# Expert down product as three fp32r products: hidden rows and down weights split in two parts, output gate weights loaded after the experts

## The reference

```
def swiglu(x, w_gate, w_up, w_down):
    return (jax.nn.silu(x @ w_gate) * (x @ w_up)) @ w_down
```

## Time and profile before

| | us |
|---|---|
| median of three runs | 1937.7 (1934.84 to 1939.48) |
| profiled execution | 1947.41 |
| its span | 1945.4 |
| PE busy | 1769.4 (91%) |
| DVE busy | 940.4 (48%) |
| ACT busy | 785.6 (40%) |
| POOL busy | 469.5 (24%) |

### The profile page before, as it was taken

How to read it: one execution, slowest core, us unless ns; L and a number is a source line. 1 busy time by engine, 2 the same in 40 slices (tenths; PEclk the granted TensorE clock), 3 DMA queues, 4 the chain that set the end, 5 groups by cost and what they waited for, 6 DMA issues and landing times. The chain is left out here.

```text
span 1945.4 us, 26491 instructions
## 1 busy us (share of the span) xinstructions
PE 1769.4 (91%) x7429; PEld 1131.6 (58%) x7430; DVE 940.4 (48%) x1605; ACT 785.6 (40%) x1460; POOL 469.5 (24%) x592
## 2 busy tenths in 40 slices
PE   7999999978997899989999988999999999866997
PEld 4666666535875666666666655666665666543443
DVE  2333333314685444554445453553555535537885
ACT  2222222212422555555555564554555545541221
POOL 0010000003662232333323323222223232320110
PEclk9999999978998999989999998999999999887999
DMA  9200000022154887887787887787888877857651
GB/s 358 76 0 0 0 0 0 24 85 98 34 132 120 256 265 225 275 282 231 239 246 237 247 252 236 236 251 225 254 245 257 257 236 216 277 194 329 258 184 38
DMA packets 158985, 358.80 MB, mean 184 GB/s; under 512 B 31858, under 2 KB 46002, under 8 KB 156365
## 3 DMA queue, kind: packets, MB, share of 16 engines
q1 hardware_dynamic: 122981, 285.78, 47.8%
q0 software_dynamic: 35328, 72.27, 10.5%
q10 hardware_dynamic: 640, 0.28, 0.1%
HBM read 330.19 MB, written 68.98 MB: 205 GB/s over the span
## 5 line engine op out<-in xcount | busy, mean ns | idle before, releaser
L194 DVE TENSOR_TENSOR lo_gu<-raw_gu,hi_gu 128x1024 fp32r<-128x1024 f32 x260 | 317.5, 1225 | 535.1 <-ACT hi_gu L188 531.5
L1257 PE MATMUL B<-raw_d,hT 128*128 128x512 f32 (+1 forms) x768 | 367.1, 630 | 55.0 <-ACT hT L1367 33.2
L188 ACT ACTIVATE hi_gu<-raw_gu 128x1024 fp32r<-128x1024 f32 x260 | 275.1, 1061 | 189.9 <-PE B L1207 189.9
L1207 PE MATMUL B<-hi_gu,x_hi 128*128 128x512 f32 (+1 forms) x768 | 327.7, 427 | 3.0 <-issue 3.0
L1093 POOL DMA_INDIRECT y_dram<-y,put x128 | 141.0, 1101 | 719.3 <-issue 376.7
L1207 PE MATMUL B<-hi_gu,x_lo 128*128 128x512 f32 (+1 forms) x768 | 304.1, 396 | 0.0
L1207 PE MATMUL B<-lo_gu,x_hi 128*128 128x512 f32 (+1 forms) x768 | 303.0, 395 | 0.0
L1257 PEld LDWEIGHTS B<-raw_d,hT 128*128 128x128 f32 (+1 forms) x768 | 138.9, 188 | 241.8 <-issue 192.4
L1353 ACT ACTIVATE y<-B 128x512 f32<-128x512 f32 (+1 forms) x256 | 146.5, 594 | 217.3 <-PE B L1257 198.7
L1207 PEld LDWEIGHTS B<-hi_gu,x_hi 128*128 128x128 f32 (+1 forms) x768 | 135.6, 177 | 60.4 <-issue 16.9
L1207 PEld LDWEIGHTS B<-lo_gu,x_hi 128*128 128x128 f32 (+1 forms) x768 | 136.1, 177 | 54.7 <-issue 13.7
(11 more groups left out here) (224 smaller groups left out, 1780.3 us busy)
## 6 DMA issues: line engine op xcount, KB each, us to landing
raw_gu<-in_w_exp_gate SPq DMA_DIRECT2D x264, 256.0 KB, 4.2
raw_gu<-in_w_exp_up SPq DMA_DIRECT2D x264, 256.0 KB, 5.3
raw_d<-in_w_exp_down SPq DMA_DIRECT2D x65, 1024.0 KB, 6.6
yk<-y_dram SPq DMA_DIRECT2D x16, 2048.0 KB, 11.8
rows_dram<-ple SPq DMA_DIRECT2D x9, 512.0 KB, 3.9
w_big<-in_w_in SPq DMA_DIRECT2D x2, 2048.0 KB, 12.5
w_out<-in_w_out SPq DMA_DIRECT2D x1, 4096.0 KB, 18.3
w_big<-in_w_ple_gate SPq DMA_DIRECT2D x64, 64.0 KB
```

The costliest lines, as they stand in the source:

```text
L188: act.activation(part_of(keep["hi_gu"], i), part_of(keep["raw_gu"][buf], i), ACT.Copy).then_inc(keep["hi_set"], 1)
L194: dve.tensor_tensor(part_of(keep["lo_gu"], i), part_of(keep["raw_gu"][buf], i), part_of(keep["hi_gu"], i).bitcast(F32), ALU.subtract).then ...
L1207: ins = pe.matmul(out, lhs[x], rhs[w], start=first and i == 0, stop=last and i == 2)
L1257: ins = pe.matmul(Y[half][0:BLK[b], :], hT[:, f, b * P:b * P + BLK[b]], raw_d[:, f, half * 512:(half + 1) * 512], start=(f == 0), stop=(f ...
```

## The change

The down product is made like the gate and up product, of three fp32r products. `raw_d` gets a second buffer (the first 2048 columns of `w_big`). ScalarE makes a high part of the next expert's down weights (`hi_d`, two buffers, also in `w_big`), between high part 3 and the copies of `y`; VectorE makes the rest (`lo_d`, one buffer) at the start of the expert that uses it, and the rest of the hidden rows (`hT_lo`). TensorE runs six fp32r matmuls for each half of a block where it ran two fp32 matmuls. SyncE loads the down weights ahead of the gate and up parts, waiting for the `lo_d` of the expert before. Since `w_big` is now in use, `w_ple_gate` is loaded whole after the last down product (4 MB, L1047), the first `g_ffn` and later router weights move to column 8192, and `w_ple_proj` is loaded after 60 experts instead of ahead of the experts.

```diff
+        if name == "g_ffn":
+            at = KC * D
...
-    raw_d, hi, lo, hi_set, lo_set, gu_ld, d_ld = (
-        keep[n] for n in ("raw_d", "hi_gu", "lo_gu", "hi_set", "lo_set", "gu_ld", "d_ld"))
+    hi, lo, hi_set, lo_set, gu_ld, d_ld, gate_ld = (
+        keep[n] for n in ("hi_gu", "lo_gu", "hi_set", "lo_set", "gu_ld", "d_ld", "gate_ld"))
+    raw_d = (keep["raw_d"][:], keep["w_big"][:, 0:FC * D].rearrange("p (f d) -> p f d", f=FC))
...
+        hT_at, hT = next_at(nc), sb("hT", [P, FC, CAP], F32R)
+        hi_d = [over(f"hi_d{b}", [P, FC, D], F32R, keep["w_big_at"] + 4 * FC * D * (3 - 2 * b)) for b in range(2)]
+        lo_d = over("lo_d", [P, FC, D], F32R, keep["w_big_at"] + 4 * FC * D * 2)
...
-            def load_down(e, m):
+            def load_down(e, m, buf):
 
                 src = a["w_exp_down"][0, e:e + 1] if isinstance(e, int) else a["w_exp_down"][0][bass.ds(e, 1)]
-                sp.wait_ge(y_done, 4 * m)
+                sp.wait_ge(lo_set, lo_count(m - 1, 0))
                 sp.sem_inc(passed, 1)
-                sp.dma_start(raw_d[:], src.rearrange("e (f p) d -> p (e f) d", p=P)).then_inc(d_ld, 16)
-
-            def load_gate_piece(n):
-                at = n * GATE_PIECE if isinstance(n, int) else sp.snap(n * GATE_PIECE)
-                sp.dma_start(keep["w_big"][:, bass.ds(at, GATE_PIECE)], gate_w[:, bass.ds(at, GATE_PIECE)]).then_inc(
-                    gate_ld, 16)
+                sp.dma_start(raw_d[buf], src.rearrange("e (f p) d -> p (e f) d", p=P)).then_inc(d_ld[buf], 16)
...
+                        load_down(sp.snap(n + 1), r * E + n + 1, (b + 1) % 2)
                         load_gate_up(sp.snap(n + 3), r * E + n + 3, (b + 1) % 2)
-                        load_down(sp.snap(n + 1), r * E + n + 1)
-                        load_gate_piece(n)
+                sp.dma_start(output_weights(keep)[1], a["w_ple_proj"][0].rearrange("(f p) d -> p f d", p=P)).then_inc(
+                    keep["output_ld"], 16)
...
+            sp.dma_start(output_weights(keep)[0], a["w_ple_gate"][0].rearrange("(p k) n -> p k n", k=KC)).then_inc(
+                gate_ld, 16)
...
-            def down(m, blocks):
-                pe.wait_ge(d_ld, 16 * m + 16)
+            def down(m, buf, blocks):
+
+                pe.wait_ge(hi_d_set, m + 1)
+                pe.wait_ge(lo_set, lo_count(m, PARTS))
                 pe.wait_ge(ht_ev, m + 1)
                 for b in range(blocks):
+                    rows_of = slice(b * P, b * P + BLK[b])
                     for half in range(2):
+                        w = slice(half * 512, (half + 1) * 512)
                         pe.wait_ge(y_ev, 4 * m + 2 * b + half + 1)
                         for f in range(FC):
-                            ins = pe.matmul(Y[half][0:BLK[b], :], hT[:, f, b * P:b * P + BLK[b]],
-                                            raw_d[:, f, half * 512:(half + 1) * 512], start=(f == 0), stop=(f == FC - 1))
+                            pe.matmul(Y[half][0:BLK[b], :], hT[:, f, rows_of], hi_d[buf][:, f, w], start=(f == 0), stop=False)
+                            pe.matmul(Y[half][0:BLK[b], :], hT[:, f, rows_of], lo_d[:, f, w], start=False, stop=False)
+                        if b == 0 and half == 0:
+                            pe.wait_ge(ht_lo_ev, m + 1)
+                        for f in range(FC):
+                            ins = pe.matmul(Y[half][0:BLK[b], :], hT_lo[:, f, rows_of], hi_d[buf][:, f, w],
+                                            start=False, stop=(f == FC - 1))
...
+            act.wait_ge(d_ld[0], 16)
+            act.activation(hi_d[0][:], raw_d[0], ACT.Copy).then_inc(hi_d_set, 1)
...
+            def down_hi(r, q, b):
+
+                act.wait_ge(d_ld[b], 16 * (E // 2) * r + 16 * q + 16)
+                act.wait_ge(y_done, 4 * E * r + 8 * q + 4 * b - 3)
+                act.activation(hi_d[b][:], raw_d[b], ACT.Copy).then_inc(hi_d_set, 1)
...
+                down_hi(r, q + b, (b + 1) % 2)
                 for half in range(2):
                     act.wait_ge(y_free, 2 * m + half + 1)
                     copy_out(m, 2 * half)
...
+            def down_lo(m, buf):
+
+                dve.wait_ge(hi_d_set, m + 1)
+                dve.wait_ge(y_done, 4 * m + 1)
+                dve.tensor_tensor(lo_d[:], raw_d[buf], hi_d[buf][:].bitcast(F32), ALU.subtract).then_inc(lo_set, 1)
+
+            def h_lo(m):
+
+                dve.wait_ge(ht_ev, m + 1)
+                dve.tensor_tensor(hT_lo[:].rearrange("p f q -> p (f q)"), HT[:, 0:FC * CAP],
+                                  hT[:].rearrange("p f q -> p (f q)").bitcast(F32), ALU.subtract).then_inc(ht_lo_ev, 1)
+
             def expert(r, n, b):
                 m = r * E + n
+                down_lo(m, b)
                 for i in range(PARTS - 1):
                     split_lo(dve, keep, (b + 1) % 2, m + 1, i)
                 hidden(m, 0)
                 hidden(m, 1)
+                h_lo(m)
...
+            pe.wait_ge(keep["gate_ld"], 16)
```

More of the change, by code:

```diff
@@ L124, in build @@
     with ExitStack() as ctx:
+        early = ExitStack()
         def sb(name, shape, dt=F32):
@@ L129, in build @@
             ident=sb("ident", [P, P]),
-            w_big=sb("w_big", [P, KC * IN_W]),
+            w_big_at=next_at(nc), w_big=sb("w_big", [P, KC * IN_W]),
             raw_gu=[sb("raw_gu0", [P, 2, KC, FE])], raw_d=sb("raw_d", [P, FC, D]),
-            **{n: ctx.enter_context(nc.semaphore(n)) for n in ("d_ld", "router_ld", "output_ld", "passed", "hi_set", "lo_set")},
-            gu_ld=[[ctx.enter_context(nc.semaphore(f"gu_ld{b}{i}")) for i in range(PARTS)] for b in range(2)],
+            **{n: ctx.enter_context(nc.semaphore(n)) for n in ("output_ld", "passed", "gate_ld")},
+            **{n: early.enter_context(nc.semaphore(n)) for n in ("router_ld", "hi_set", "lo_set")},
+            d_ld=[early.enter_context(nc.semaphore(f"d_ld{b}")) for b in range(2)],
+            gu_ld=[[early.enter_context(nc.semaphore(f"gu_ld{b}{i}")) for i in range(PARTS)] for b in range(2)],
         )
@@ L149, in build @@
             moe(nc, a, c, keep, rows_dram, y_dram, list_dram)
+        early.close()
         output(nc, a, o, keep, y_dram)
@@ L883, in moe @@
         half = sb("half2", [P, 1])
-        place = sb("place", [P, 2 * AHEAD + 1, E])
+        place_at, place = next_at(nc), sb("place", [P, 2 * AHEAD + 1, E])
         base = sb("base", [P, E])
         biased = sb("biased", [P, E])
+        hT_lo = over("hT_lo", [P, FC, CAP], F32R, place_at)
         top2 = sb("top2", [P, EG, 8])
@@ L902, in moe @@
         sums = sb("sums", [P, 2])
-        sT = hT[0:E, 0, 0:P]
+        sT = over("sT", [E, P], F32, hT_at)[:]
         top = sb("top", [1, 2])
@@ L970, in _ @@
                 store_rows(t)
-            sp.dma_start(raw_d[:], a["w_exp_down"][0, 0].rearrange("(f p) d -> p f d", p=P)).then_inc(d_ld, 16)
+            sp.dma_start(raw_d[0], a["w_exp_down"][0, 0].rearrange("(f p) d -> p f d", p=P)).then_inc(d_ld[0], 16)
             for i in range(PARTS):
                 load_part(sp, a, keep, 1, 1, i)
-            sp.dma_start(output_weights(keep)[1], a["w_ple_proj"][0].rearrange("(f p) d -> p f d", p=P)).then_inc(
-                ple_ld, 16)
             for b in range(2):
@@ L1265, in expert @@
                 h_transposes(m, blocks)
-                down(m, blocks)
+                down(m, b, blocks)
             def lists(r):
@@ L1357, in expert @@
                 m, j = r * E + n, r * NJ + n + 1
-                act.activation(warm[:], warm[:], ACT.Sigmoid).then_inc(warmed, 1)
+                act.activation(warm[:], warm[:], ACT.Sigmoid).then_inc(passed, 1)
                 for i in range(PARTS - 1):
```

32 lines of the change are left out of this document (19 added, 13 removed).

## The result

The changed kernel takes 1962.16 us (median of 4 runs, 1960.90 to 1967.57) where the one before takes 1937.69: a ratio of 1.0133, interval 1.011 to 1.0156. It is slower by 24.5 us; I had forecast 1900, and 1868 to 1938 as the range. Its profiled execution takes 1962.79 us, near its median; the one of before lies 9.7 above its own, so between the two profiles there are only 15.4 us (spans 1960.8 and 1945.4).

A forecast was written before the change was run, and what follows sets the result against it. TensorE was taken to set the expert stage's pace, busy 1033 of 1106 us, with about 59 us lost in one-block chains. Terms 0 - 11 - 30 + 1 + 2 = -38 gave 1937.7 - 38 = 1900, range 1868 to 1938.

The forecast's parts named there:

- Part 1: Down-product matmuls: six fp32r in 1.39 replace 1.71 per half-block; -0.64 per one-block expert, -1.28 per two-block, -61 if all on path.
- Part 2: Cast on ACT before copies of y: two-block experts 0, one-block behind two-block -11, one-block behind one-block +7.
- rival C: New 1.5 us wait in each two-block down product drops the clock: +89, 1989; chance 0.08.
- the +7 for the chains: One-block experts behind one-block ones: the cast delays hidden rows, raising the floor 0.45 each, times 15.
- Part 3: Split on DVE: lo_d (2.3 us) and the rest of hT (0.59) stay hidden, 0; without cover at most 38.
- part 4: Earlier down-weight load: -33 for waits and clock, POOL's share -4; with +7, -30 for 15 one-block experts behind one-block ones.
- The -33: Nine TensorE waits for down weights go, 19.0, with half of the 26 lost to half clock behind them, 14.
- part 5: Start and end: +1 for a load beside the first rows, +2 for y loads overlapping 4 MB of gate weights.
- -30: Sum for the 15 one-block experts behind one-block ones; bounds -48 and +7.
- Rival B: One-block chains stay bound by transfers, DMA 0.80 busy, POOL's waits replacing the 33: -1, 1937; chance 0.12.
- Rival E: lo_d holds POOL's two list copies in one-block chains, up to 2.3 us an expert: +34, 1934; chance 0.05.

The follow-up runs named there:

- two scatters in flight: Changed kernel with POOL no longer waiting for an expert's first scatter ahead of its second: 1902.44 us; the same edit on the kernel before: 1916.61 us.
- the fp32 product: Fp32 down product of the kernel before, with second buffer and earlier down load, both scatters in flight, gate weights behind first y loads: 1892.16 us.
- the early load alone: Changed kernel with the down product back in plain fp32, keeping the second down-weight buffer, its earlier load and the late gate-weight load: 1940.14 us.
- load in mid-expert: Changed kernel with the down weights loaded behind gate and up part 1, for the expert two ahead: 1926.08 us.
- scatters and cast between: Changed kernel with both scatters of an expert in flight and ScalarE's cast between the second and third copy of y: 1903.27 us.
- cast split: Changed kernel with both scatters in flight, down load in mid-expert, gate weights behind first y loads, cast halves behind first and second copy: 1877.69 us.
- cast and rest split: The kernel with the split cast, with VectorE's low part of the down weights also made in two halves; the fastest version: 1856.87 us.

## Why the prediction was wrong

**Right.** Part 1: a half-block takes 1.40 (778.78 to 780.18 in the changed kernel's timeline) for the 1.39 forecast; a one-block expert behind a two-block one takes 0.4 less (median 11.68 for 12.05), where 0.64 was forecast. Part 2: the two-block experts stay at 21.0 (20.90), since the cast in front of the copies eats the gain, and the clock doesn't fall behind that wait (rival C): it is 1.00 through the two-block expert above, from 747.6 to 768.5. But the +7 for the chains isn't seen: with two scatters in flight most chain experts take 11.9, less than the 12.1 of the fp32 product, and what lifts the mean to 12.71 is four slow ones. Part 3: nothing shows on the path in the changed kernel; once the chains run faster the low part of the down weights does (the wait of 1.0 that became 0.7 when it was split).

**The step that failed** is part 4, "I let POOL's share of the loss fall by 4". The -33 beside it, nine waits and the half clock behind them, is about the right size: with the early load alone the ten experts concerned take 32 less (the tenth stands behind the 1690 us at which the earlier trace rows ends). But POOL's share rose: +13 in the other five, where I had -4. Its two scatters an expert each wait for the landing of the last, some 8 us each. As I read it, the first chain expert's wait for down weights had given POOL time to catch up; without that wait the expert behind it waits for its rows. I read the table of waits as a list of sums; what a second engine's lateness will cost once a wait is gone isn't in it. It shows only in what POOL itself waited for (its scatters sat 376.7 us behind what the page calls issue). Neither edit alone brings the chains of the kernel before to their floor: the early load takes 1.3 off each, two scatters in flight 1.8, both together 3.6, to 12.1.

**The second step** is in the same part: I counted the earlier load as a wait removed and hadn't asked what else goes out at that moment. Its new place is beside the first scatter of a two-block expert, so that POOL comes late into the chain, and even the ten stay where they were (154.0 for 153.2). When the load is moved again, the chain experts take 1.4 less each, the two-block experts behind them 0.55, and the kernel 36.

**The third** is a term of part 5: I put the end at +2 for y loads that share the queues with the gate weights; it is 7.3, because it's the last scatters that share with them and the barrier waits for those (-7.5 when moved).

In sum, from the profiles: forecast -38, measured +15.4, 53 apart. The chains make 32 of it (+2.0 for -30), the two-block experts behind them 8, the one-block ones behind two-block 6, the end 5, and the start with the first expert 3, less 2 that the other two-block experts gained. Of the chains' 32, POOL's series makes 17 (early load alone) and the collision 21 (load in mid-expert), less some 6 of the +7 that didn't come.

Rival B came nearest: its sign, waits for rows or for POOL over 40 in sum, came with 110. But it priced the chain as unchanged and so stopped at 1937, and the reason that it gave, DMA 0.80 busy, isn't the bound: the fastest version here moves the same weights at 263 GB/s for 241. Rival E is seen but not on the path: POOL's `put` copy took 1.36 beside the 2.36 of `lo_d`, and then POOL waited 2.04 for ACT all the same. The rule of the Trainium skill's page "SBUF — State Buffer", section "Who interferes with whom", that I had named agrees with the 1.36, and no run here tells its price alone.

Open: why before's runs spread so much (1927 to 1953 over all sessions) I haven't shown.

## What to carry to other kernels

Before a wait's time is counted as a gain, follow the other engines through the same stretch and the next: if a serial chain (a gather, a scatter, a landing, the next scatter) takes as long as the expert does, the wait is what lets it catch up, part of the gain comes back as another wait, and the cheap change is to put two transfers in flight. When a transfer is moved, look at what else goes out within a microsecond of it. And a large cast on an engine that also empties the banks is best cut into pieces between the copies.

## What the hardware showed

A scatter of 128 rows of 4 KB, followed by the next in 5.3 us, took until 10.4 beside a 1 MB load issued within 0.2 us of it, and 13.6 beside one of 4 MB (4.4 with that one moved away). A cast of 128x2048 took 1.93 on ScalarE, the subtraction 2.29 on VectorE, close to the 2.0 and 2.3 worked out from the narrower ones. A wait of 0.84 in the middle of a down product left the granted clock at 1.00 in the two-block experts. In the 15 chain experts of each run, waits of some 1.8 for the hidden rows were followed by the lower level of the clock in 13 (scatters and cast between), waits of some 1.0 in 8 (cast split), and waits of some 0.65 in 2 (cast and rest split).
